# Two input matrices laid out by features on the host, row factors spread by products, and the residual input loaded late

## The chip, the cores and the metric

One core of one Trainium2 chip runs the whole program. The metric is the device time of one execution in microseconds (us); each version is run several times and the median is given.

## The reference

Two transformer blocks with T = 256 tokens and D = 1024 features run one after the other, in fp32. The change touches the opening of the first block only:

```python
hx = modulate(rms_norm(x, norm1_g[i]), sh1, sc1)      # x   [256, 1024]
hc = modulate(rms_norm(ctx, norm1_g[i]), csh1, csc1)  # ctx [256, 1024]
qx, kx, vx, ux = split_proj(hx @ w_in[i])
kvc = hc @ w_in[i][:, ATT_DIM:3 * ATT_DIM]
...
x_new = x + g1 * (jnp.concatenate([attn_x, conv_x], axis=-1) @ w_out[i])
```

`rms_norm` divides each token's row by the root of its mean square and multiplies by a gain per feature; `modulate(h, shift, scale)` is `h * (1 + scale) + shift`, where shift and scale come from `silu(c) @ w_ada + b_ada` (for ctx from c_ctx). So a token needs one factor (the "row factor") and a feature needs a factor and an addend.

## The kernel before

The program is one hand-written instruction stream per engine, tied by counting semaphores; an engine runs its own stream strictly in the order written. SyncE (`sync_program`) issues the weight loads through one queue in the order of `weight_units`, each when the ring slots that it overwrites have been read. TensorE (PE) multiplies. Weights are split in two fp32r parts: ScalarE (ACT) writes the high part WH (`high_halves`, called `hi`), VectorE (DVE) the low part WL (`low_halves`, called `lo`), and every product is three matmuls: high x high, high x WL, low activations x WH. The activations are split likewise into AH and AL (for x) and CH and CL (for ctx).

The opening works so. SyncE loads x by tokens (X, two blocks of 128 tokens on the partitions), then for e8 = 0 to 7 an 1 MB block of w_ada ("ada block") and a 0.5 MB block of w_in ("ab block"); ctx (XC) goes into the queue between ab block 6 and ada block 7; after ab block 7 follow the 1 MB blocks k0, k1, q0, q1, v0, v1. k0 may be issued when PE has read ada block 5, k1 when it has read ada block 7. ACT squares the rows of X with a sum along the row, GpSimd (POOL) raises mean + eps to -0.5 (`power`), DVE multiplies X by the row factor (`hat`) into S1. PE first runs 11 filler products of ones (`keep_busy`, L476, each two instructions), then `mod_first(0)` (L454, the ada product), `mod_turn(0)` (L465 transposes 2 blocks of S1, L468 the 2 row blocks of the modulation), 8 more filler products, and then the loop over e8: `mod_first(e8 + 1)`, `ab(e8, 0)`, `mod_turn(e8 + 1)`, `ab(e8, 1)` (L490 to L496). For each e8 DVE copies the modulation rows out (`rows_out`), sums and adds (`modulation`), applies factor and addend to the turned S1 in PSUM (`modulate_x`, L1538), writes WL of the ab block, and AL (`low_x`); ACT copies AH (`high_x`).

For ctx ACT squares XC after e8 = 5, DVE scales it (`hat`, L1493) into XC2 at e8 = 6 and once more between the low parts of k0 and k1. PE turns XC2 by `c_turns` (L396), twice two banks of four transposes, between the parts of the k product. DVE (`modulate_c0`) and ACT (`modulate_c(1)` to `(3)`, L1033) apply factor and addend out of PSUM.

Behind this DVE goes on in written order: low parts of q0 and q1, rope of K (KR), 20 taps of the depthwise convolution (L1496), low parts of v, 8 taps, rope of Q (QR, after ACT has copied Q out), 52 taps, and then the attention loop over u = 0 to 7. There `soft1` (L1666) adds bias and finds maxima, ACT takes the exponential, `norm1` (L1493) scales, PE turns the probabilities (`turn1`, L396), and `pv1(u)` (L598) multiplies by V into bank 5. `pv1(u)` takes that bank only when DVE has run `o1_lo(u - 1)` (L1490). In its loop DVE runs norm1(u), soft1 of u + 1, the tail of the modulation, some taps, then o1_lo(u - 1). Before `turn1(0)` PE runs the second half of the last v product, scores1(1) and two ada products.

Of the kernel before, what the change touches and what calls it, by code (L numbers as in the profile page):

```python
# [5 lines left out]
F32 = mybir.dt.float32  # L6
# [18 lines left out]
class Mem:  # L25


    def __init__(self, nc, ctx):
# [30 lines left out]
        def M(name, off, shape, dt=F32):  # L59
            return at(name, 121.75 + off, shape, dt)  # L60
# [10 lines left out]
        self.XC2 = M("XC2", 56, [128, 2, D])  # L71
# [69 lines left out]
x_hat mx_dve mx_act kx c_hat c_turned mc_dve mc_act kc  # L141
# [143 lines left out]
def sync_program(e, m, S, units, out, d):  # L285
    w = Waits(e)

    def load(n):
        unit = units[n]
        for old in unit.old:  # L290
            w.wait_ge(old.free[0], old.free[1])
        v = unit.block(m)
        for c0, cw, src in unit.pieces:
            e.dma_start(v[:, :, c0:c0 + cw], src).then_inc(unit.landing, 16)

    for tb in range(2):
        e.dma_start(m.X[:, tb, :], d["x"][128 * tb:128 * tb + 128, :]).then_inc(S[f"l_x{tb}"], 16)
    for n in range(14):
        load(n)
    e.dma_start(m.XC[:, :, :], d["ctx"].rearrange("(t p) n -> p t n", p=128)).then_inc(S["l_xc"], 16)  # L300
    for n in range(14, len(units)):
        load(n)
    for n in range(3):
        tb, c = n // 2, slice(512 * (n % 2), 512 * (n % 2) + 512)
        e.wait_ge(S["y_out"], n + 1)
        e.dma_start(out[tb * 128:tb * 128 + 128, c], m.S1[:, tb, c]).then_inc(S["l_out"], 16)
    e.wait_ge(S["l_out"], 64)
# [58 lines left out]
def tensor_program(e, m, S, by):  # L366
# [11 lines left out]
    def frees(b, *pairs):  # L378
        free[b] = [(S[sem], value) for sem, value in pairs]
# [79 lines left out]
    def mod_turn(e8):  # L459

        b = turn_bank("rows1_turned")
        w.wait_ge(S["l_id"], 16)
        w.wait_ge(S["x_hat"], 2)
        for tb in range(2):
            e.transpose(bank[b][:, 256 + tb * 128:384 + tb * 128], m.S1[:, tb, 128 * e8:128 * e8 + 128], m.ident[:, :])  # L465
        w.wait_ge(S["rows1_dve"], e8 + 1)
        for j in range(2):
            ins = e.transpose(bank[b][:, j * 128:j * 128 + 128], m.rows1[e8][:, j * 128:j * 128 + 128], m.ident[:, :])  # L468
        ins.then_inc(S["rows1_turned"], 1)
        frees(b, ("mx_dve", e8 + 1))  # L470
# [10 lines left out]
    def ab(e8, tb):  # L481

        unit = by["ab"][e8]
        wh, wl = m.WH[unit.slot], m.WL[unit.slot]
        hs = m.AH[:, e8, tb * 128:tb * 128 + 128]
        ls = m.AL[:, e8, tb * 128:tb * 128 + 128]
        w.wait_ge(S["mx_act"], e8 + 1)
        for n in range(2):
            w.wait_ge(S["w_hi"], unit.hi + n + 1)
            e.matmul(bank[2 * n + tb][:, :], hs, wh[:, 512 * n:512 * n + 512], start=e8 == 0, stop=False)  # L490
        for n in range(2):
            w.wait_ge(unit.lo[0], unit.lo[1] + n + 1)
            e.matmul(bank[2 * n + tb][:, :], hs, wl[:, 512 * n:512 * n + 512], start=False, stop=False)
        w.wait_ge(S["kx"], e8 + 1)
        for n in range(2):
            e.matmul(bank[2 * n + tb][:, :], ls, wh[:, 512 * n:512 * n + 512], start=False,  # L496
                     stop=e8 == 7).then_inc(S["b_mm" if n else "a_mm"], 1)

    keep_busy(11)
    mod_first(0)  # L500
    mod_turn(0)
    keep_busy(8)
    for e8 in range(8):
        if e8 < 7:
            mod_first(e8 + 1)
        ab(e8, 0)
        if e8 < 7:
            mod_turn(e8 + 1)
        ab(e8, 1)
    for tb in range(2):  # L510
        frees(tb, ("u", tb + 1))
        frees(2 + tb, ("gate_u", tb + 1))

    def c_turn(i):
        w.wait_ge(S["c_hat"], 2)
        b = turn(pair(m.XC2, 2 * i), "c_turned")
        frees(b, ("mc_act", 3 * i - 1) if i else ("mc_dve", 2))
# [6 lines left out]
    def c_turns(i):  # L524
        c_turn(i)
        c_turn(i + 1)

    def u_turns():
        u_turn(0)
# [3 lines left out]
    def c_ready(k):  # L533
        return "kc", k // 2 + 1

    product(by["k"], m.AH, m.AL, 0, 4, "k_mm", x_ready, 512, lambda: c_turns(0))
    frees(4, ("k_out", 1))
    c_turns(2)
    product(by["k"], m.AH, m.AL, 1, 5, "k_mm", x_ready, 512, u_turns)
    frees(5, ("k_out", 2))  # L540
    for tb in range(2):
# [447 lines left out]
def scalar_program(e, m, S, units, by, out, d):  # L989
# [32 lines left out]
    def high_x(k):  # L1022

        w.wait_ge(S["mx_dve"], k + 1)
        copy(m.AH[:, k, :], m.hT[:, k, :], "mx_act")

    def modulate_c(i, n):

        w.wait_ge(S["c_turned"], i + 1)
        w.wait_ge(S["mod1"], 16)  # L1030
        for k in (2 * i, 2 * i + 1):
            src = bank[m.turn_bank["c_turned", i + 1]][:, k % 2 * 256:k % 2 * 256 + 256]
            e.activation(m.hTc[:, k, :], src, ACT.Identity, bias=m.mod1[:, k, 0, 1:2],  # L1033
                         scale=m.A1[:, 1, k:k + 1]).then_inc(S["mc_act"], 1)
# [429 lines left out]
def vector_program(e, m, S, units, by):  # L1464
# [33 lines left out]
    def col(i):  # L1498
        return stat[:, i:i + 1]
# [777 lines left out]
```

## Time and profile before

| | us |
|---|---|
| median of 3 runs | 733.89 (733.76 to 734.76) |
| the profiled execution | 736.95 |
| its span | 735.1 |
| PE busy in the span | 722.5 |
| DVE busy in the span | 508.5 |
| ACT busy in the span | 397.8 |

All times of rows below are microseconds from the start of the span of the profiled execution. That execution took 3.06 us more than the median. PE stands still for 12.6 us in all, so the rows tell most at the few places where it does and where it nearly does.

### The profile page before, as it was taken

How to read it: one execution, taken by the hardware profiler on the slowest of the kernel's cores; microseconds unless marked ns; L12 is line 12 of the kernel's file. 1: busy time of each engine (PE TensorE's matmuls, PEld its weight loads, DVE VectorE, ACT ScalarE, POOL GpSimd, SP SyncE). 2: the span in 40 equal slices, each digit the busy share in tenths (PEclk: the TensorE clock that was granted, in tenths of full speed). 3: DMA queues.
4: the chain of work that ended last, by engine and by line, in shares of the span. 5: the costliest groups of instructions: out<-in, count | busy, mean ns of one | idle time of the engine just before them, and what ended most of it. 6: DMA issues, size and time to landing. Idle time of an engine off the chain costs nothing.

```text
span 735.1 us, 9749 instructions
## 1 busy us (share of the span) xinstructions
PE 722.5 (98%) x3806; PEld 577.7 (79%) x3806; DVE 508.5 (69%) x924; ACT 397.8 (54%) x662; POOL 24.9 (3%) x44
## 2 busy tenths in 40 slices
PE   7999999999999999999999999999999999999996
PEld 5668885568888888888878777778888888888885
DVE  3688999889667555565988799865857445544544
ACT  3366336886666545556545677666466344434432
POOL 1020011000100000000010000000000000000000
PEclk8999999999999999999999999999999999999999
DMA  9984939954464656545528533344366655655511
GB/s 366 385 325 172 364 114 357 370 171 165 162 221 167 229 182 215 172 157 190 160 96 302 203 116 115 118 171 170 115 230 203 197 173 189 206 177 171 173 58 57
DMA packets 73741, 144.90 MB, mean 197 GB/s; under 512 B 4112, under 2 KB 27664, under 8 KB 72672
## 3 DMA queue, kind: packets, MB, share of 16 engines
q1 hardware_dynamic: 71888, 138.98, 54.6%
q0 software_dynamic: 1520, 5.03, 1.9%
q8 instruction: 30, 0.49, 0.3%
q10 hardware_dynamic: 288, 0.27, 0.1%
q14 instruction: 15, 0.12, 0.0%
HBM read 143.22 MB, written 1.05 MB: 196 GB/s over the span
## 4 chain that ended last, share of the span: by engine, by line
PE 92%; DVE 3%; issue 2%; DMA 1%; ACT 1%; POOL 0%; SPq 0%; POOLq 0%; DVEq 0%
PE bank L414 22%; PE bank L416 22%; PE bank L415 22%; PE bank L734 5%; PE bank L396 5%; PE bank L732 3%; PE bank L433 2%; PE bank L454 1%; DMA W<-in_w_ada 1%; PE bank L576 1%; PE bank L490 1%; PE bank L598 1%; PE bank L851 1%; PE bank L873 1%; DVE WL L1481 1%
## 5 line engine op out<-in xcount | busy, mean ns | idle before, releaser
L1481 DVE TENSOR_TENSOR WL<-W,WH 128x1024 fp32r<-128x1024 f32 (+2 forms) x222 | 249.5, 1169 | 47.7 <-ACT WH L1004 47.4
L1004 ACT ACTIVATE WH<-W 128x1024 fp32r<-128x1024 f32 (+2 forms) x222 | 211.5, 1011 | 52.8 <-DMA W<-in_w_mlp 40.3
L414 PE MATMUL bank<-WH,AHL 128*128 128x512 f32 (+1 forms) x480 | 189.2, 394 | 0.3 <-DVE AHL L1490 0.3
L416 PE MATMUL bank<-WH,AHL 128*128 128x512 f32 (+1 forms) x480 | 185.4, 386 | 0.0
L415 PE MATMUL bank<-WL,AHL 128*128 128x512 f32 (+1 forms) x480 | 185.2, 386 | 0.0
L414 PEld LDWEIGHTS bank<-WH,AHL 128*128 128x128 f32 x480 | 90.2, 188 | 21.5 <-issue 3.2
L416 PEld LDWEIGHTS bank<-WH,AHL 128*128 128x128 f32 x480 | 90.2, 188 | 18.7
L415 PEld LDWEIGHTS bank<-WL,AHL 128*128 128x128 f32 x480 | 90.3, 188 | 16.9
L414 PE MATMUL bank<-WH,HH 128*128 128x512 f32 (+1 forms) x218 | 84.9, 390 | 0.0
L416 PE MATMUL bank<-WH,HL 128*128 128x512 f32 (+1 forms) x218 | 84.5, 388 | 0.0
L415 PE MATMUL bank<-WL,HH 128*128 128x512 f32 (+1 forms) x218 | 84.4, 387 | 0.0
L734 PE MATMUL bank<-AHL,WH 128*128 128x512 f32 x168 | 60.5, 398 | 0.0
L732 PE MATMUL bank<-AHL,WL 128*128 128x256 f32 x192 | 50.0, 281 | 0.0
L1496 DVE SCALAR_TENSOR_TENSOR cacc<-hp,vec,cacc 128x256 f32<-128x256 f32 x120 | 48.3, 475 | 0.0
L416 PEld LDWEIGHTS bank<-WH,HL 128*128 128x128 f32 x218 | 40.9, 188 | 8.5
L415 PEld LDWEIGHTS bank<-WL,HH 128*128 128x128 f32 x218 | 41.0, 188 | 8.3
L414 PEld LDWEIGHTS bank<-WH,HH 128*128 128x128 f32 x218 | 40.9, 188 | 8.0
L1413 ACT ACTIVATE rel<-bank 128x256 f32<-128x256 f32 x22 | 8.5, 384 | 62.2 <-PE bank L416 61.1
L1490 DVE TENSOR_TENSOR hid<-bank,rel 128x256 f32<-128x256 f32 x22 | 9.3, 424 | 42.2 <-ACT rel L1413 42.2
L732 PEld LDWEIGHTS bank<-AHL,WL 128*128 128x128 f32 x192 | 36.3, 189 | 2.0
L734 PEld LDWEIGHTS bank<-AHL,WH 128*128 128x128 f32 x168 | 31.6, 188 | 6.7
L1784 DVE TENSOR_TENSOR HL<-bank,HH 128x256 fp32r<-128x256 f32 (+1 forms) x26 | 11.1, 460 | 30.9 <-ACT HH L1012 30.9
(265 smaller groups left out, 829.5 us busy)
## 6 DMA issues: line engine op xcount, KB each, us to landing
W<-in_w_mlp SPq DMA_DIRECT2D x32, 1024.0 KB, 5.4
W<-in_w_in SPq DMA_DIRECT2D x24, 1024.0 KB, 5.1
W<-in_w_ada SPq DMA_DIRECT2D x12, 1024.0 KB, 7.5
WX<-in_w_ada SPq DMA_DIRECT2D x12, 1024.0 KB, 9.4
W<-in_w_gate SPq DMA_DIRECT2D x22, 512.0 KB, 4.1
W<-in_w_up SPq DMA_DIRECT2D x22, 512.0 KB, 5.3
W<-in_w_down SPq DMA_DIRECT2D x11, 1024.0 KB, 4.9
W<-in_w_out SPq DMA_DIRECT2D x8, 1024.0 KB, 5.0
```

The source lines that it names most:

```text
L396: ins = e.transpose(bank[b][:, c * 128:c * 128 + 128], src, m.ident[:, :])
L414: e.matmul(po, hs, wh[:, k, c0:c0 + cw], start=first and k == 0, stop=False)
L415: e.matmul(po, hs, wl[:, k, c0:c0 + cw], start=False, stop=False)
L416: ins = e.matmul(po, ls, wh[:, k, c0:c0 + cw], start=False, stop=last and k == unit.nk - 1)
L433: ins = e.matmul(bank[bk][32 * g:32 * g + 32, :], m.csp[:, k0 + g, :], wv[:, g, :], start=k0 == 0, stop=k0 == 4, tile_position=(0, 32 * g))
L732: ins = e.matmul(bank[4 + j][:, 0:256], wl[:, k, js], m.AH[:, 4 * i + k, :], start=False, stop=False)
L734: ins = e.matmul(both, wh[:, k, js], m.AHL[:, :, 4 * i + k, :], start=False, stop=i == 1 and k == 3)
L1004: e.activation(m.WH[unit.slot][:, c], m.W32[unit.slot][:, c], ACT.Copy).then_inc(S["w_hi"], 1)
L1481: e.tensor_tensor(m.WL[unit.slot][:, c], m.W32[unit.slot][:, c], m.WH[unit.slot][:, c].bitcast(F32), ALU.subtract).then_inc(S["w_lo"], 1)
L1490: e.tensor_tensor(o, a, b, op).then_inc(S[sem], 1)
L1496: e.scalar_tensor_tensor(o, a, scalar, b, op0, op1).then_inc(S[sem], 1)
L1784: e.tensor_tensor(L[:, k0:k0 + nj, ts], bank[b][:, 0:nj * 128].rearrange("p (j n) -> p j n", j=nj), H[:, k0:k0 + nj, ts].bitcast(F32), ALU ...
```

## The change

x and ctx are also laid out by features on the host (XT and CT: 128 partitions, 8 blocks, 256 tokens). At the start XT is loaded in two halves instead of X. ACT squares XT elementwise (no sum), and PE sums the squares over features by products with a column of ones: 16 products with one output column (`x_sums`), then `spread` brings the two row factors over all partitions by 2 products with the identity, and DVE copies them to rB. `modulate_x` reads XT and rB from SBUF and multiplies by factor and row factor; the addend is put in by ACT in `high_x` and by DVE in `low_x`. The two transposes of S1 in each `mod_turn` are gone. The filler is 6 products before x_sums, 4 between x_sums and spread, and 4 (was 8) behind mod_turn(0).

For ctx, XC still comes by tokens for the squares, and CT is loaded as well, between ab block 7 and k0. DVE's two scalings (`hat`) go; instead DVE, behind `u`, multiplies CT by the spread factors in PSUM (two operations of 128 x 1024), and `modulate_c0` and `modulate_c` read CT from SBUF. The four `c_turn`s of four transposes are gone from PE; one `spread` is added between ab(7, 0) and ab(7, 1). X by tokens is loaded behind v1, and `residual1` waits for it.

```diff
-    for tb in range(2):
-        e.dma_start(m.X[:, tb, :], d["x"][128 * tb:128 * tb + 128, :]).then_inc(S[f"l_x{tb}"], 16)
+    for h in range(2):
+        e.dma_start(m.XT[:, 4 * h:4 * h + 4, :], d["xt"][:, 4 * h:4 * h + 4, :]).then_inc(S[f"l_x{h}"], 16)
...
     for n in range(14, len(units)):
+        if n == 16:
+            e.dma_start(m.CT[:, :, :], d["ctxt"]).then_inc(S["l_ct"], 16)
+        if n == 22:
+            e.dma_start(m.X[:, :, :], d["x"].rearrange("(t p) n -> p t n", p=128)).then_inc(S["l_x"], 16)
         load(n)
...
-        w.wait_ge(S["x_hat"], 2)
-        for tb in range(2):
-            e.transpose(bank[b][:, 256 + tb * 128:384 + tb * 128], m.S1[:, tb, 128 * e8:128 * e8 + 128], m.ident[:, :])
...
-    keep_busy(11)
+    def x_sums():
+
+        for h in range(2):
+            w.wait_ge(S["sq_sum"], h + 1)
+            for k in range(4 * h, 4 * h + 4):
+                for tb in range(2):
+                    ins = e.matmul(bank[6 + tb][:, 0:1], m.xsq[:, k, tb * 128:tb * 128 + 128], m.ones[:, 0:1], start=k == 0,
+                                   stop=k == 7)
+        ins.then_inc(S["r_mm"], 1)
+
+    def spread(b, i):
+
+        w.wait_ge(S["l_id"], 16)
+        w.wait_ge(S["rstd"], i + 2)
+        for tb in range(2):
+            ins = e.matmul(bank[b][:, tb * 128:tb * 128 + 128], m.stat[:, 40 + i + tb:41 + i + tb].to_broadcast([128, 128]),
+                           m.ident[:, :], start=True, stop=True)
+        ins.then_inc(S["r_mm"], 1)
+
+    keep_busy(6)
+    x_sums()
+    keep_busy(4)
+    spread(turn_bank("x_spread", 6), 0)
+    frees(6, ("r_x", 1))
     mod_first(0)
     mod_turn(0)
-    keep_busy(8)
+    keep_busy(4)
...
+        else:
+            b = turn_bank("c_spread")
+            spread(b, 2)
+            frees(b, ("c_hat", 2))
...
-    product(by["k"], m.AH, m.AL, 0, 4, "k_mm", x_ready, 512, lambda: c_turns(0))
+    product(by["k"], m.AH, m.AL, 0, 4, "k_mm", x_ready)
     frees(4, ("k_out", 1))
-    c_turns(2)
     product(by["k"], m.AH, m.AL, 1, 5, "k_mm", x_ready, 512, u_turns)
...
-        copy(m.AH[:, k, :], m.hT[:, k, :], "mx_act")
+        e.activation(m.AH[:, k, :], m.hT[:, k, :], ACT.Identity, bias=m.mod1[:, k, 0, 0:1]).then_inc(S["mx_act"], 1)
...
-        square(tb, m.X[:, tb, :], m.S1[:, tb, :])
+        e.activation(half_of(m.xsq, tb), half_of(m.XT, tb), ACT.Square, scale=1.0 / 32).then_inc(S["sq_sum"], 1)
...
         if k == 6:
             mean_square(2, (2,))
-            hat(m.XC, m.XC2, 0, 2, "c_hat")
-    lo()
-    mean_square(3, (3,))
-    hat(m.XC, m.XC2, 1, 3, "c_hat")
-    lo()
+            mean_square(3, (3,))
+    lo(2)
     for tb in range(2):
         w.wait_ge(S["gate_u"], tb + 1)
         w.wait_ge(S["a_mm"], 15 + tb)
         tt(m.U[:, tb, :], bank[tb][:, :], m.G[:, tb, :], ALU.mult, "u")
+    w.wait_ge(S["r_mm"], 3)
+    w.wait_ge(S["l_ct"], 16)
+    for i in range(2):
+        cv = m.CT[:, 4 * i:4 * i + 4, :]
+        rv = bank[m.turn_bank["c_spread", 1]][:, 0:256]
+        tt(cv, cv, rv.unsqueeze(1).to_broadcast([128, 4, 256]), ALU.mult, "c_hat")
     modulate_c0()
```

## Rows read from the trace of the kernel before

**Rows 1.** The page, part 1: busy time and share of the span.

```profile
PE 722.5 (98%) x3806; PEld 577.7 (79%) x3806; DVE 508.5 (69%) x924; ACT 397.8 (54%) x662; POOL 24.9 (3%) x44
```

**Rows 2.** Windows: stretch, PE, PEld, DVE, ACT, POOL busy, PEclk, DMA share, GB/s.

```profile
9.00:10.00 1.00, 0.42 (x5) 0.26 (x9) 0.00 (x0) 0.00 (x0) 0.00 (x0) 0.54 1.09 451
...
15.00:16.00 1.00, 1.00 (x6) 0.85 (x5) 0.46 (x2) 0.67 (x2) 0.00 (x0) 0.55 0.94 385
...
42.00:46.00 4.00, 3.61 (x30) 2.12 (x28) 3.06 (x7) 2.95 (x5) 0.55 (x1) 1.00 0.37 93
```

**Rows 3.** Timeline of PE, opening: start, duration, engine, line, operation.

```profile
9.57 1.94 PE L454 MATMUL bank<-W,csp 128*32 128x256 f32 x16 [2.72 <-DMA W<-in_w_ada]
...
12.53 3.56 PE L476 MATMUL bank<-ones 128*128 128x128 f32 x16
```

**Rows 4.** Timeline of ACT, the second square of X.

```profile
5.42 1.04 ACT L1016 ACTIVATE S<-X 128x1024 f32<-128x1024 f32 x1
```

**Rows 5.** Timeline of POOL, the power of one row factor.

```profile
5.85 0.56 POOL L317 TENSOR_TENSOR stat<-stat 128x1 f32<-128x1 f32 x1 [3.15 <-DVE stat L1507]
```

**Rows 6.** The chain of waits: start, us on the chain, what.

```profile
53.84 0.87 PE bank L396 x8
...
155.97 0.54 PE bank L639 x4
```

**Rows 7.** Timeline of PE: ada block 7, ab(7, 0), k product, turn1(0), pv1(1).

```profile
42.52 1.07 PE L454 MATMUL bank<-WX,csp 128*32 128x256 f32 x16
...
47.90 0.73 PE L490 MATMUL bank<-WH,AHL 128*128 128x512 f32 x2 [0.29 <-ACT AHL L1012]
...
50.95 0.40 PE L414 MATMUL bank<-WH,AHL 128*128 128x512 f32 x1
...
115.91 1.09 PE L396 MATMUL bank<-ident,s 128*128 128x128 f32 x8
...
125.37 0.66 PE L598 MATMUL bank<-PT,V 128*64 128x128 f32 x8
```

**Rows 8.** Timeline of DVE from U to o1_lo(0).

```profile
54.87 1.28 DVE L1490 TENSOR_TENSOR U<-bank,G 128x512 f32<-128x512 f32 x2
...
67.08 1.22 DVE L1490 TENSOR_TENSOR KR<-Kt,rope 128x1024 f32<-128x1024 f32 x1 [0.20 <-ACT Kt L1012]
...
87.14 1.23 DVE L1490 TENSOR_TENSOR QR<-Q,rope 128x1024 f32<-128x1024 f32 x1 [0.60 <-ACT Q L1012]
...
90.88 20.68 DVE L1496 SCALAR_TENSOR_TENSOR cacc<-hp,vec,cacc 128x256 f32<-128x256 f32 x52
...
114.47 0.49 DVE L1493 TENSOR_SCALAR s<-s,rl 128x512 f32<-128x512 f32 x1
...
124.94 0.28 DVE L1490 TENSOR_TENSOR AHL<-bank,AHL 128x128 fp32r<-128x128 f32 x1
```

**Rows 9.** Timeline of ACT: WH of k0 and k1, modulate_c(3), WH of q0 and q1.

```profile
47.76 3.89 ACT L1004 ACTIVATE WH<-W 128x1024 fp32r<-128x1024 f32 x4
...
59.54 1.01 ACT L1033 ACTIVATE hTc<-bank,mod,A 128x256 f32<-128x256 f32 x2
...
61.11 3.89 ACT L1004 ACTIVATE WH<-W 128x1024 fp32r<-128x1024 f32 x4
```

**Rows 10.** DMA issues one by one, us to landing: ada block 7, k0, k1.

```profile
WX<-in_w_ada SPq DMA_DIRECT2D x1, 1024.0 KB, 10.6
...
W<-in_w_in SPq DMA_DIRECT2D x1, 1024.0 KB, 9.8
...
W<-in_w_in SPq DMA_DIRECT2D x1, 1024.0 KB, 5.1
```

**Rows 11.** Timeline of SyncE's queue and one issue's source: when issued.

```profile
30.23 0.47 SPq L294 DMA_DIRECT2D WX<-in_w_ada  x1
...
L294 SPq DMA_DIRECT2D W<-in_w_in x1: 379/379/379, 34.9 to 34.9; - x1
...
L294 SPq DMA_DIRECT2D W<-in_w_in x1: 379/379/379, 43.7 to 43.7; - x1
```

More of the change, by code:

```diff
@@ L70, in __init__ @@
         self.XC = M("XC", 48, [128, 2, D])
-        self.XC2 = M("XC2", 56, [128, 2, D])
+        self.CT = M("CT", 56, [128, 8, 256])
+        self.XJ = M("XJ", 64, [128, 2, D])
+        self.XT = M("XT", 0, [128, 8, 256])
+        self.xsq = M("xsq", 24, [128, 8, 256])
+        self.rB = M("rB", 72, [128, 256])
         self.hTc = M("hTc", 0, [128, 8, 256])
@@ L140 @@
 sq_sum mean_sq rstd ada1_mm rows1_dve rows1_turned mod1_sum mod1
[L141 removed]
+r_mm r_x l_x l_ct mx_dve mx_act kx c_hat mc_dve mc_act kc
 a_mm b_mm gate_u u u_turned hp conv_first conv k_mm q_mm v_mm k_out kc_out q_out v_out vc_out rope_mul kr qr qk_turned qk_act
@@ L469, in mod_turn @@
         ins.then_inc(S["rows1_turned"], 1)
-        frees(b, ("mx_dve", e8 + 1))
+        frees(b, ("mod1_sum", e8 + 1))
     def keep_busy(count):
@@ L512, in tensor_program @@
         frees(2 + tb, ("gate_u", tb + 1))
[L514 to L517, printed above, removed]
     def u_turn(j):
@@ L522, in u_turn @@
         frees(b, ("hp", j + 1))
-    def c_turns(i):
-        c_turn(i)
-        c_turn(i + 1)
     def u_turns():
@@ L1024, in high_x @@
         w.wait_ge(S["mx_dve"], k + 1)
-        copy(m.AH[:, k, :], m.hT[:, k, :], "mx_act")
+        e.activation(m.AH[:, k, :], m.hT[:, k, :], ACT.Identity, bias=m.mod1[:, k, 0, 0:1]).then_inc(S["mx_act"], 1)
     def modulate_c(i, n):
-        w.wait_ge(S["c_turned"], i + 1)
-        w.wait_ge(S["mod1"], 16)
+        w.wait_ge(S["c_hat"], 2)
+        w.wait_ge(S["mx_dve"], 8)
         for k in (2 * i, 2 * i + 1):
-            src = bank[m.turn_bank["c_turned", i + 1]][:, k % 2 * 256:k % 2 * 256 + 256]
-            e.activation(m.hTc[:, k, :], src, ACT.Identity, bias=m.mod1[:, k, 0, 1:2],
+            e.activation(m.hTc[:, k, :], m.CT[:, k, :], ACT.Identity, bias=m.mod1[:, k, 0, 1:2],
                          scale=m.A1[:, 1, k:k + 1]).then_inc(S["mc_act"], 1)
@@ L1039, in two, with half_of @@
         return hT[:, 2 * i:2 * i + 2, :].rearrange("p a b -> p (a b)")
+    def half_of(t, h):
+        return t[:, 4 * h:4 * h + 4, :].rearrange("p a b -> p (a b)")
     e.dma_start(m.cs[:, :], d["cs"]).then_inc(S["l_cs"], 16)
@@ L1051, in scalar_program @@
     for tb in range(2):
-        square(2 + tb, m.XC[:, tb, :], m.XC2[:, tb, :])
+        square(2 + tb, m.XC[:, tb, :], m.XJ[:, tb, :])
     hi()
@@ L1537, in modulate_x @@
         w.wait_ge(S["mod1"], 2 * k + 2)
-        e.tensor_scalar(m.hT[:, k, :], bank[m.turn_bank["rows1_turned", k + 1]][:, 256:512], m.A1[:, 0, k:k + 1],
-                        m.mod1[:, k, 0, 0:1], ALU.mult, ALU.add).then_inc(S["mx_dve"], 1)
+        w.wait_ge(S["r_x"], 1)
+        w.wait_ge(S[f"l_x{k // 4}"], 16)
+        fused(m.hT[:, k, :], m.XT[:, k, :], m.A1[:, 0, k:k + 1], m.rB[:, :], ALU.mult, ALU.mult, "mx_dve")
     def low_x(k):
@@ L1544, in low_x @@
         w.wait_ge(S["mx_act"], k + 1)
-        tt(m.AL[:, k, :], m.hT[:, k, :], m.AH[:, k, :].bitcast(F32), ALU.subtract, "kx")
+        fused(m.AL[:, k, :], m.hT[:, k, :], m.mod1[:, k, 0, 0:1], m.AH[:, k, :].bitcast(F32), ALU.add, ALU.subtract, "kx")
     def modulate_c0():
         w.wait_ge(S["mod1"], 16)
-        w.wait_ge(S["c_turned"], 1)
+        w.wait_ge(S["c_hat"], 2)
         for k in range(2):
-            e.tensor_scalar(m.hTc[:, k, :], bank[m.turn_bank["c_turned", 1]][:, k * 256:k * 256 + 256], m.A1[:, 1, k:k + 1],
+            e.tensor_scalar(m.hTc[:, k, :], m.CT[:, k, :], m.A1[:, 1, k:k + 1],
                             m.mod1[:, k, 0, 1:2], ALU.mult, ALU.add).then_inc(S["mc_dve"], 1)
@@ L1566, in vector_program @@
     e.tensor_copy(m.csp[:, :, 0:2], m.cs[:, :].rearrange("p (k r) -> p k r", r=2)).then_inc(S["csp"], 1)
+    w.wait_ge(S["r_mm"], 1)
     for tb in range(2):
-        mean_square(tb, (tb,))
-        hat(m.X, m.S1, tb, tb, "x_hat")
+        e.tensor_scalar(col(24 + tb), bank[6 + tb][:, 0:1], EPS, None, ALU.add).then_inc(S["mean_sq"], 1)
+    w.wait_ge(S["r_mm"], 2)
+    e.tensor_copy(m.rB[:, :], bank[6][:, 0:256]).then_inc(S["r_x"], 1)
     for k in range(8):
@@ L1792, in residual1 @@
         hn = slice(512 * n, 512 * n + 512)
+        w.wait_ge(S["l_x"], 16)
         w.wait_ge(S["out_mm"], OUT_AT[n, tb])
@@ L2230, in fm, with blocks @@
         return v.reshape(-1, 128).T
+    def blocks(v):
+        return v.T.reshape(8, 128, 256).transpose(1, 0, 2)
     bada = a["b_ada"].reshape(-1)
@@ L2260 @@
     arrays = {
-        "vec": vec, "cs": cs, "x": a["x"][0], "ctx": a["ctx"][0], "ident": np.eye(128, dtype=np.float32),
+        "vec": vec, "cs": cs, "x": a["x"][0], "ctx": a["ctx"][0], "xt": blocks(a["x"][0]), "ctxt": blocks(a["ctx"][0]), "ident": np.eye(128, dtype=np.float32),
         "rope1": rope_tables(lambda t: (t // 64, t % 64), 32), "rope2": rope_tables(lambda t: (t,), 64),
```

## Prediction

> **What bounds the kernel now.** I read the page's busy times first: PE works 722.5 us of 735.1 [rows 1], so an edit pays only if it takes work off PE or closes one of its few holes, and only as long as no other engine becomes late. Then I read the timelines of PE, ACT, POOL and DVE over the first 126 us, with the windows for clock and DMA. The opening shows a hole of 2.72 us before the first ada product, which waits for its block [rows 3]; within it the granted clock falls to 1.2 GHz (0.54 is the mean of the microsecond from 9, so it fell at 9.1), and it is back at 2.4 GHz from 15.9 (0.55 from 15 to 16) [rows 2]. From there PE is busy to 111 us but for 0.39 us between 42 and 46 [rows 2] and 0.29 before 47.9 [rows 7], 0.7 together. What the page doesn't tell is how late the other engines are. DVE starts the attention stage directly out of its 52 taps, which run from 90.88 for 20.68 us, that is to 111.56 [rows 8]. Its first normalised probabilities are ready at 114.47 + 0.49 = 114.96; PE turns them at 115.91 [rows 7, 8]: 0.95 us of slack. Its o1_lo(0) ends at 124.94 + 0.28 = 125.22, and pv1(1), which needs it, starts at 125.37 [rows 7, 8]: 0.15 us. So at 125 us DVE is as much the bound as PE, and whatever PE gains before is kept only as far as DVE comes earlier too. That is the core of this forecast.
>
> **The change on PE.** Gone at 2.4 GHz: 16 transposes of S1 and 16 of ctx. Eight cost 0.87 us [rows 6], 0.109 each: 3.5 us, of which the pair in mod_turn(0) ran at 1.2 GHz and cost twice. Gone at 1.2 GHz: 4 of 8 filler products, 3.56/8 = 0.445 each [rows 3], 1.8 us. Gone as well are 0.7 us of holes at e8 = 7 behind the scaling of XC. Added: one spread at e8 = 7, 4 instructions of 0.109, 0.45 us, and the opening's 16 one-column products. Each is 2 instructions; four such instructions (L639) took 0.54 us with their tail [rows 6], the transposes say 0.109: 32 cost 3.5 to 4.3 us at 2.4 GHz, double at 1.2. The second half starts only when ACT's second square is done at 5.42 + 1.04 = 6.5 [rows 4]; the first half may not be through by then.
>
> The opening, at 2.4 GHz throughout: one-column products end near 9.1; DVE adds eps, POOL takes two powers of 0.56 [rows 5], about 10.5; spread 0.45; the first ada product starts at 10.9 (was 9.57), but takes 1.0 instead of 1.94, and with 4 fast filler products the second starts at 13.6 (was 16.02). At e8 = 1 PE is 2.6 us ahead, and each step gives 0.22 more. By e8 = 7 it wants ada block 7 at 38.1 (was 42.52 [rows 7]). That block was issued at 30.23 and landed at 40.8 [rows 10, 11], and the DMA engines are full in the opening (a share of 0.94 to 1.09, 385 to 451 GB/s [rows 2]), so it can't come much sooner: 40.2 I take. The rest of the loop takes 50.95 - 42.52 = 8.43 us less the 0.7 of holes and 0.22, plus 0.45: 8.0. PE reaches the k product at 48.2 (was 50.95), waits a little for k0's low part (48.6), and loses the four c_turns: 2.35 + 1.74 = 4.1 us ahead until turn1(0).
>
> **The change on DMA, ACT and DVE.** CT puts 1 MB ahead of k0. Between 42 and 46 us only 93 GB/s flowed [rows 2], at 400 that leaves room for 1.2 MB, so CT fills a hole: k0 (issued at 34.9, landed 44.7 [rows 10, 11]) comes about 2 us later, k1 (43.7, landed 48.8 [rows 10, 11]) about when it did. Its issue waits for ada block 7's product and so moves up 2.3 us, while the hole in front is gone: between 48.2 (all of the hole used) and 51.4 (CT's 2.6 us added in full); I take 48.5. X, another 1 MB, is issued behind v1 and so lies in front of nothing but the later ada blocks; at the start XT's 1 MB takes X's place. Both cost nothing.
>
> ACT needs 0.97 us for each half of k1 [rows 9], so its high part is ready at 50.45 (was 51.65). DVE's last low part takes 1.2, as KR's product of the same size does [rows 8]: 51.65. U: 1.28 for two [rows 8]: 52.9. Now the new operations: CT times factors, 128 x 1024 with one operand in PSUM, twice. U costs 0.64 for 512 elements a partition, so 1.28 for one at most, and 1.22 at least, which KR's product of 1024 elements took out of SBUF; I take 2.45 in all: 55.4. This is added to the chain, since ACT's three modulate_c, which began at 54.76 before, now wait for it. One takes 61.11 - 59.54 = 1.57 [rows 9], with CH behind; three 4.75: ACT begins q0's high part at 60.15 (was 61.11). DVE's two old scalings and its waits for POOL's powers are gone, which is why DVE isn't later. The fused forms of modulate_x and low_x are the operation of the taps at the same size, 20.68/52 = 0.40 each [rows 8]; I cost them at nothing, the loop over e8 hides them while it waits for its block, and 0.1 each would move A by less than 0.1. All later steps of DVE follow ACT by the old distance: KR at 66.1 (was 67.08 [rows 8]). QR waited 0.60 for ACT's copy of Q [rows 8]; PE is 4.1 us early there, so that wait goes.
>
> **Sum.** DVE at 111.5: 0.95 + 0.60 = 1.55 us earlier. At turn1(0) PE may gain 1.55 + 0.95 = 2.5; at pv1(1) 1.55 + 0.15 = 1.7. PE has 4.1, so it stands about 1.6 us before turn1(0) and 0.8 more by pv1(1), and **1.7 us** is what is left. Behind this PE's steps are longer than DVE's, the slack grows, and the gain stays. The profiled execution would take 736.95 - 1.7 = 735.25; the median, 3.06 lower, 732.2.
>
> **The rivals.** (A, forecast, 0.42) As above, 732.2, with k1's landing and the two products with the factors as unknowns: 731.3 to 732.9.
>
> (B, 0.32) The opening stays at 1.2 GHz for longer. There is less filler, one-column products keep PE little occupied, and before 9 us the clock was lost while PE stood [rows 2, 3]. Then the spread and the first ada product cost double, the first starts at 11.7, ends at 13.6, and e8 = 0 is done 1 to 2 us later than it was; ada block 7 is asked for near 42, k1 is issued at 43 and lands at 49.5. DVE is then 0.55 early at 111.5, the gain is 0.7: 733.2. The clock of 10 to 20 us decides between A and B. The Trainium skill (TensorE: Matmul & The Clock Gate, Part 1) says that "the default state is throttled, and activity releases the throttle". By that rule taking filler out speaks for B; the rows agree in that the clock fell in the hole and came back behind eight filler products.
>
> (C, 0.06) DVE isn't the bound I take it for; PE keeps all of its 4.1 us: 729.8. Against it stands the slack of 0.15 us [rows 7, 8].
>
> (D, 0.11, slower) The new hole before turn1(0), 1.6 us here and more if DVE comes later, takes the clock down, as the hole of 2.72 us did [rows 3], and PE runs at 1.2 GHz for a stretch as long as then, 6.8 us from 9.1 to 15.9 [rows 2]. That costs half of it, 3.4 us, on a PE-bound stage: -1.7 + 3.4 = +1.7, 735.6. It decides once the hole comes near the old one's length.
>
> (E, 0.09, slower) CT doesn't fit into the hole, k1 lands at 51.4. All of ACT's and DVE's chain is 2.9 us later than in A: 735.1. It turns into a loss from a landing at 50.2 on.
>
> **How the numbers follow.** A measurement of this kernel can tell 0.2% from no change, 1.47 us; the limits are 732.4 and 735.4. A reaches to both sides of the lower limit: 0.30 of its 0.42 below it. Faster 0.30 + 0.06 and 0.02 from B: 0.38. Slower: D and half of E, with a little for costs that I have not seen, 0.18. The rest, 0.44, is no change. The range takes in A, B and E and the cheaper end of D: 731.0 to 735.4.
>
> **What would show it.** Right: ada block 7's product waits for its block near 40; k1 lands at 48 to 49.5; the new products of DVE lie at about 53 to 55.4 with 1.17 to 1.28 each; ACT starts q0's high part near 60; QR without a wait; PE idle before turn1(0) with DVE as the releaser, and again before pv1(1). Wrong: PE without a hole at 112 us, DVE at its taps until 111.5 or later, a clock under 1.0 behind 20 us, or k1's landing past 50. If the opening is at 1.2 GHz to 19 us, B holds.

## The result: 7.4 us slower, and the profile after

The changed kernel takes 741.25 us (median of 4 runs, 740.38 to 743.04) against 733.86 (733.76 to 734.76): a ratio of 1.0098, 95% interval 1.0085 to 1.0111. The forecast was 732.2, its range 731.0 to 735.4. The profiled execution took 741.68 us, its span is 739.9. That is 4.7 us more than the profiled one of before (736.95), which was itself 3.06 above its median.

The page after, parts 1 and 4 (the chain's share of the span by engine); before, PE's share of the chain was 92% and DVE's 3%.

```profile
PE 726.8 (98%) x3804; PEld 581.2 (79%) x3804; DVE 508.3 (69%) x923; ACT 398.6 (54%) x660; POOL 24.6 (3%) x44
...
PE 82%; DVE 11%; ACT 3%; issue 2%; DMA 1%; POOL 0%; POOLq 0%; DVEq 0%; SPq 0%
```

PE executes two instructions fewer and is busy 4.3 us longer; DVE's part of the chain has grown fourfold. PE's timeline after, opening and attention stage:

```profile
2.76 2.93 PE L481 MATMUL bank<-ones 128*128 128x128 f32 x12 [2.76 <-POOL ones L342]
6.12 6.99 PE L510 MATMUL bank<-ones,xsq 128*128 128x1 f32 x32 [0.43 <-ACT xsq L1070]
12.97 2.05 PE L481 MATMUL bank<-ones 128*128 128x128 f32 x8
...
15.81 1.94 PE L462 MATMUL bank<-W,csp 128*32 128x256 f32 x16
...
20.69 1.92 PE L462 MATMUL bank<-WX,csp 128*32 128x256 f32 x16
...
25.76 1.07 PE L462 MATMUL bank<-W,csp 128*32 128x256 f32 x16
...
119.80 1.09 PE L404 MATMUL bank<-ident,s 128*128 128x128 f32 x8 [1.74 <-DVE s L1517]
...
130.15 0.66 PE L620 MATMUL bank<-PT,V 128*64 128x128 f32 x8 [0.30 <-DVE AHL L1514]
```

The first ada product starts at 15.81 (was 9.57), the second at 20.69 (was 16.02, behind the 3.56 us of filler [rows 3]). Both take 1.9 us, the third 1.07: PE ran at 1.2 GHz up to some 22.5 us, and no fall follows before the last 5 us of the span. The windows' PEclk column says 1.00 all through that opening, since it knows no earlier level than the first recorded change; the durations of equal work tell the level.

DVE and ACT after, from U to turn1(0)'s source; the answering rows are [rows 8, 9]:

```profile
55.79 2.36 DVE L1505 TENSOR_TENSOR WL<-W,WH 128x1024 fp32r<-128x1024 f32 x2 [0.86 <-ACT WH L1026]
58.07 1.28 DVE L1514 TENSOR_TENSOR U<-bank,G 128x512 f32<-128x512 f32 x2
59.27 2.34 DVE L1514 TENSOR_TENSOR CT<-CT,bank 128x1024 f32<-128x1024 f32 x2
...
72.57 1.23 DVE L1514 TENSOR_TENSOR KR<-Kt,rope 128x1024 f32<-128x1024 f32 x1 [0.19 <-ACT Kt L1034]
...
91.94 1.22 DVE L1514 TENSOR_TENSOR QR<-Q,rope 128x1024 f32<-128x1024 f32 x1
...
95.67 20.67 DVE L1520 SCALAR_TENSOR_TENSOR cacc<-hp,vec,cacc 128x256 f32<-128x256 f32 x52
...
119.25 0.49 DVE L1517 TENSOR_SCALAR s<-s,rl 128x512 f32<-128x512 f32 x1
```

```profile
54.70 2.01 ACT L1026 ACTIVATE WH<-W 128x1024 fp32r<-128x1024 f32 x2 [1.21 <-DMA W<-in_w_in]
...
61.64 1.09 ACT L1054 ACTIVATE hTc<-CT,mod,A 128x256 f32<-128x256 f32 x2 [3.96 <-DVE CT L1514]
...
66.60 3.89 ACT L1026 ACTIVATE WH<-W 128x1024 fp32r<-128x1024 f32 x4
```

The reader is to see three steps. ACT waits for k1 until 54.70, where it had landed at 48.8 [rows 10, 11]: 5.9 later. 4.2 of them come from ada block 7's product, which k1's issue waits for and which starts at 46.75 instead of 42.52 [rows 7]; the other 1.7 go with CT ahead of k1 in the queue (tested below). So U starts 3.2 later than before. The two products with the factors add 2.34, so KR is 5.5 late. QR no longer waits (it had 0.60), the taps are 4.8 late, and turn1(0), which had 0.95 of slack, is 3.9 late and waits 1.74 for DVE. From its start to the end of the span it is another 620.1, before 619.2 [rows 7]; two more new waits, 0.48 before an ada product and the 0.30 before pv1(1), make up nearly all of that difference.

### The profile page after: what moved, and what is told of

Read it like the earlier page. It is cut to its first block, busy times and chain, and to the rows that moved or that the text cites. A ratio compares the mean times of both kernels' runs of the same rounds, so it can differ in the third digit from the quotient of the medians.

```text
span 739.9 us, 9751 instructions
## 1 busy us (share of the span) xinstructions
PE 726.8 (98%) x3804; PEld 581.2 (79%) x3804; DVE 508.3 (69%) x923; ACT 398.6 (54%) x660; POOL 24.6 (3%) x44
## 4 chain that ended last, share of the span: by engine, by line
PE 82%; DVE 11%; ACT 3%; issue 2%; DMA 1%; POOL 0%; POOLq 0%; DVEq 0%; SPq 0%
PE bank L422 20%; PE bank L424 19%; PE bank L423 19%; PE bank L756 5%; DVE cacc L1520 5%; PE bank L404 4%; PE bank L754 3%; DVE WL L1505 1%; PE bank L462 1%; PE bank L441 1%; PE bank L510 1%; PE bank L495 1%; DMA W<-in_w_in 1%; PE bank L873 1%; PE bank L895 1%
```

## The experiments

Theory at the start: (1) the opening at 1.2 GHz costs most; (2) DVE, not PE, carries the delay into the attention stage; (3) CT and its products add to DVE's chain. Rivals: the freed hole and its clock (D), and that PE alone sets the time. The kernel before was measured again beside each group of experiments (734.05 to 734.24 us); the ratios are to that. The name in brackets behind a result is the one by which later expectations call the version.

### Sums with 128 output columns

```diff
-                    ins = e.matmul(bank[6 + tb][:, 0:1], m.xsq[:, k, tb * 128:tb * 128 + 128], m.ones[:, 0:1], start=k == 0,
+                    ins = e.matmul(bank[6 + tb][:, 0:128], m.xsq[:, k, tb * 128:tb * 128 + 128], m.ones[:, 0:128], start=k == 0,
```

> The changed kernel with one size altered: the 16 products that sum the squares multiply by 128 columns of ones instead of 1 (same number of instructions and of weight loads). Theory (the one-column products don't count as work for the clock, so PE stays at 1.2 GHz until 22.5 us, and everything starts late): the clock rises during or soon after these products, which then take 3.5 to 5 us instead of 6.99, the first ada product starts near 12 to 13.5 (15.81), DVE's 52 taps start 2 to 4 us earlier than 95.67, and the time falls by 2 to 4 us against the changed kernel. Rival (the shorter filler ahead of them lost the clock, the columns don't matter): the clock still rises at 22 us and the time is that of the changed kernel within 0.7 us.

Measured (e1_wide): 736.92 us (736.37 to 739.54, 10 runs), 1.0034 of before (1.0023 to 1.0045): 4.3 less than the changed kernel, a little more than the 2 to 4 expected. PE's timeline of this kernel, and two windows (PEclk is the number ahead of the last two):

```profile
6.11 3.85 PE L510 MATMUL bank<-ones,xsq 128*128 128x128 f32 x32 [0.42 <-ACT xsq L1070]
...
12.15 1.07 PE L462 MATMUL bank<-W,csp 128*32 128x256 f32 x16
...
15.09 1.07 PE L462 MATMUL bank<-WX,csp 128*32 128x256 f32 x16
...
114.38 1.09 PE L404 MATMUL bank<-ident,s 128*128 128x128 f32 x8 [2.13 <-DVE s L1517]
```

```profile
115.00:116.00 1.00, 1.00 (x9) 0.74 (x9) 1.00 (x4) 1.00 (x3) 0.77 (x2) 0.69 1.06 397
117.00:119.00 2.00, 2.00 (x12) 0.20 (x8) 2.00 (x6) 0.93 (x2) 0.00 (x0) 0.55 1.05 388
```

The 32 instructions took 3.85 us, and the first ada product is 3.7 us earlier, at full clock. DVE's 52 taps start at 90.25, 5.4 earlier (expected 2 to 4). Nine of its ten executions lie within 1 us. So the larger part of the loss lies in the opening. Rival D's mechanism appears too: a hole of 2.13 us, then 1.2 GHz from 115.4 to 118.8.

### More filler, or far fewer one-column products

```diff
-    keep_busy(6)
+    keep_busy(11)
```

> The changed kernel with the 11 filler products of the kernel before ahead of the sums instead of 6. Rival (filler was what the clock lacked): the clock rises near 6 us as in the kernel before, the one-column products take 3.5 us, the time falls by 2 to 4 us. Theory (one-column products don't count): the clock may rise at the end of the filler but falls again during the one-column products, which start at 6.9 to 7.6 us; the first ada product starts between 13 and 17 us, and the time changes by less than 1.5 us.

Measured (e2_filler): 738.63 us (737.09 to 738.75, 4 runs), 1.0045 (1.0028 to 1.0062), 2.6 less than the changed kernel. PE's opening and a window:

```profile
7.62 3.90 PE L510 MATMUL bank<-ones,xsq 128*128 128x1 f32 x32
...
14.23 1.43 PE L462 MATMUL bank<-W,csp 128*32 128x256 f32 x16
...
12.00:14.00 2.00, 2.00 (x10) 1.87 (x9) 0.00 (x0) 0.25 (x1) 0.96 (x2) 0.50 1.03 422
```

With the clock up from 8.2, soon after they began, the one-column products take 3.90 us, inside the 3.5 to 4.3 of the forecast. But behind them, with PE busy throughout, the clock is down from 11.6 to 15.0. The theory had this fall right and the time wrong: it allowed less than 1.5 us, and the 2.6 lie in the rival's 2 to 4. So the shorter filler is part of the cause beside the one-column products; with it back the clock came up at 8.2 instead of 22.5.

In the next one DVE adds the eight blocks first, and PE needs only 2 one-column products:

```diff
...
+        w.wait_ge(S["xs"], 5)
+        for tb in range(2):
+            ins = e.matmul(bank[6 + tb][:, 0:1], m.xsq[:, 0, tb * 128:tb * 128 + 128], m.ones[:, 0:1], start=True, stop=True)
```

> The changed kernel, but DVE, which idles there, adds the 8 feature blocks of the squares first (5 additions, about 1.6 us of them behind ACT's last square), and PE needs 2 one-column products instead of 16. Theory (the 7 us of the sums stand on the path of the opening): the sums end near 10 us (13.11), the first ada product starts at 12 to 13 (15.81), DVE's 52 taps start about 3 us earlier than 95.67, and the time falls by about 3 us. Rival (the opening is hidden behind the loads of the ada blocks): the time falls by less than 1 us.

Measured (e3_presum): 737.46 us (736.37 to 738.68, 8 runs), 1.0039 (1.0027 to 1.0051). PE waits 3.58 us for DVE, and its first ada product still runs at 1.2 GHz:

```profile
9.27 1.01 PE L508 MATMUL bank<-ones,xsq 128*128 128x1 f32 x4 [3.58 <-DVE xsq L1511]
...
12.99 1.92 PE L462 MATMUL bank<-W,csp 128*32 128x256 f32 x16
```

It is 3.8 us faster than the changed kernel although PE stands idle: the 7 us of slow instructions cost more than a hole of 3.58.

### Is DVE the bound? Narrow taps, in both kernels

```diff
+            cw = 128 if 36 <= n < 84 else 256
-            fused(m.cacc[:, c, :], m.hp[:, c, j:j + 256], m.dw[:, c, j:j + 1], m.cacc[:, c, :], ALU.mult, ALU.add, "conv")
+            fused(m.cacc[:, c, 0:cw], m.hp[:, c, j:j + cw], m.dw[:, c, j:j + 1], m.cacc[:, c, 0:cw], ALU.mult, ALU.add, "conv")
```

> The changed kernel with 48 of the 52 taps before the attention stage on 128 of their 256 columns (so half of these taps' work is left out and the convolution is not the reference's): some 6.4 us less work for DVE between 95.7 and 116. Theory (behind the opening DVE alone carries the delay into the attention stage; PE is only 2.1 us late at its turns of K and Q, 104.7 against 102.63): the hole of 1.74 us before turn1(0) goes, PE is the bound, and the time falls by 2.3 to 3.0 us. Rival (DVE's taps lie beside work that is as late): the time falls by less than 1 us.

48 of the 52 taps leave out half of their columns, so the convolution isn't the reference's. Measured in the changed kernel (e4_narrow): 737.29 us (737.13 to 738.98, 6 runs), 4.0 less (expected 2.3 to 3.0). DVE's taps take 14.27 instead of 20.67, and turn1(0) no longer waits:

```profile
94.41 14.27 DVE L1520 SCALAR_TENSOR_TENSOR cacc<-hp,vec,cacc 128x256 f32<-128x256 f32 x52
...
116.36 1.09 PE L404 MATMUL bank<-ident,s 128*128 128x128 f32 x8
```

Not all of it is DVE's: in this execution the clock was up from 17.4, and PE reached the turns of K at 103.08, after 104.71 in the changed kernel. Of the 4.3 between the two profiled executions 1.6 belong to the opening, and 1.74 + 0.48 + 0.30 = 2.5 are the waits that went. The clock didn't fall behind turn1(0).

> The kernel before with 48 of the 52 taps on 128 of 256 columns, as in e4_narrow (half of these taps' work left out). It says what 6.4 us less of DVE's work is worth where the opening isn't late. Theory (in the kernel before PE and DVE are level at the attention stage, slack 0.15 to 0.95 us): the time changes by less than 0.7 us, so the 4.0 us that the same cut gave in the changed kernel are lateness that DVE carried. Rival (DVE bounds the kernel before as well): the time falls by over 2 us.

The same edit in the kernel before (e8_narrow_before): 735.37 us (733.79 to 737.09, 10 runs), 1.001 (0.9998 to 1.0021). The median is 1.3 above before's, outside the 0.7 expected; the profiled execution (735.39) had its clock down from 10.4 to 13.8 in the opening, and from turn1(0)'s start to the end of its span it takes 619.2, as before. 6.4 us off DVE bring nothing where PE isn't waiting for it. The pair shows that DVE bounds the changed kernel and not the one before.

### The hole before turn1(0)

On top of the wide sums, 8 filler products stand in the hole:

```diff
+        if n == 0:
+            fb = 6 + turns["n"] % 2
+            take(fb)
+            for _ in range(8):
+                e.matmul(bank[fb][:, 0:128], m.ones[:, :], m.ones[:, :], start=True, stop=True)
```

> The kernel of e1_wide with 8 filler products (1.8 us at 2.4 GHz) in the hole before turn1(0), into the bank that turn1(0) writes next. In e1_wide PE stood 2.1 us there and the clock was at 1.2 GHz from 115.4 to 118.8. Theory (the hole takes the clock down, and that costs half of the 3.4 us): no stretch at 1.2 GHz behind 20 us, the time falls by 1.2 to 1.8 us against e1_wide (736.9), to about 735.4. Rival (PE at 1.2 GHz there waits for DVE anyway): the time stays within 0.5 us of e1_wide.

Measured (e5_hole): 736.17 us (735.85 to 739.44, 10 runs), 1.0039 (1.0024 to 1.0053). By the medians that is 0.75 less than without the filler; by the ratios (1.0039 for 1.0034) it isn't less, since four of the ten executions are slow for another reason. The clock stays up behind the filler. With PE no longer slowed, pv1(1) waits for DVE where it had no wait. And the opening of the profiled execution (738.77) is a slow one, though its sums have 128 columns:

```profile
6.19 6.60 PE L510 MATMUL bank<-ones,xsq 128*128 128x128 f32 x32 [0.50 <-ACT xsq L1075]
...
127.25 0.66 PE L625 MATMUL bank<-PT,V 128*64 128x128 f32 x8 [0.29 <-DVE AHL L1519]
```

What the fall costs is read from the profiled executions. From turn1(0)'s start to the end of the span they take 619.2 to 619.3 us without a hole (before, and five experiments), 620.1 with a hole, or the filler in it, and the clock kept (the changed kernel, this one and one below), and 620.7 to 620.8 with a hole and the clock down (four). So the fall costs about 0.7, not the 3.4 that rival D charged and not the 1.2 to 1.8 expected here: a PE that waits for DVE anyway loses little by being slow. As to the opening, six of the ten executions lie between 735.85 and 736.25, four between 738.77 and 739.44. With the 739.54 of the version without the filler, five of twenty executions with wide sums are some 3 us slower than the rest, and with one-column sums seven of eight (the x part alone, below). So wide sums seem to make the slow opening rarer; they don't exclude it. Only one of the five was profiled.

### Each half alone

The kernel before with the ctx part only (`CT` ahead of k0, one `spread`, no `c_turns`):

```diff
+        if n == 16:
+            e.dma_start(m.CT[:, :, :], d["ctxt"]).then_inc(S["l_ct"], 16)
...
-    product(by["k"], m.AH, m.AL, 0, 4, "k_mm", x_ready, 512, lambda: c_turns(0))
+    product(by["k"], m.AH, m.AL, 0, 4, "k_mm", x_ready)
     frees(4, ("k_out", 1))
-    c_turns(2)
```

> The kernel before with the part on ctx alone (CT loaded between ab block 7 and k0, DVE multiplies it behind U, no c_turns, one spread); x is as before. Theory (DVE's new 2.34 us and the later k blocks are on the chain that leads through the taps into the attention stage, PE's 1.74 us are not): DVE's 52 taps start later than in the kernel before by 1 to 2.5 us, a hole opens before turn1(0), the time is 735 to 737.5, slower than before. Rival (all of the loss comes from x's sums in the opening): the time is 732 to 734.

Measured (e6_c_only): 735.73 us (735.02 to 739.2, 11 runs) against 734.05, 1.0014 (1.0004 to 1.0024): 1.7 slower by the medians, 0.3 to 1.8 by the interval. The profiled execution is the slowest, 739.2: PE ran at 1.2 GHz up to about 15.5, though the opening is the old one. Its second ada product starts at 15.83, that of before's profile at 16.02, so the rows of the two can be compared. ACT's timeline, two rows of DVE, and the windows in which the hole of before lay [rows 2]:

```profile
51.50 2.01 ACT L1010 ACTIVATE WH<-W 128x1024 fp32r<-128x1024 f32 x2 [2.57 <-DMA W<-in_w_in]
...
58.45 1.10 ACT L1038 ACTIVATE hTc<-CT,mod,A 128x256 f32<-128x256 f32 x2 [3.97 <-DVE CT L1495]
...
52.59 2.36 DVE L1486 TENSOR_TENSOR WL<-W,WH 128x1024 fp32r<-128x1024 f32 x2 [2.20 <-ACT WH L1010]
54.87 1.28 DVE L1495 TENSOR_TENSOR U<-bank,G 128x512 f32<-128x512 f32 x2
...
42.00:44.00 2.00, 2.00 (x21) 1.02 (x20) 2.00 (x7) 1.76 (x3) 0.14 (x1) 1.00 1.02 402
44.00:46.00 2.00, 2.00 (x13) 1.65 (x12) 0.66 (x4) 1.19 (x3) 0.92 (x2) 1.00 0.88 254
```

CT does flow into the hole: 402 and 254 GB/s where 93 had been the mean. Yet k1 comes at 51.5 where 48.8 had been: 2.7 later, the time of 1 MB at 390 GB/s. ada block 7's product starts no later here (42.31 for 42.52). That is the landing of rival E (51.4). Still U starts at 54.87, just as before [rows 8]: DVE's two scalings are gone, and the wait of 2.20 for k1 takes the time that they left free. The two products behind U, 2.34, then come on top, and KR starts 2.3 later than before.

The x part only (the changed kernel with ctx as before):

```diff
-        if n == 16:
-            e.dma_start(m.CT[:, :, :], d["ctxt"]).then_inc(S["l_ct"], 16)
...
-    product(by["k"], m.AH, m.AL, 0, 4, "k_mm", x_ready)
+    product(by["k"], m.AH, m.AL, 0, 4, "k_mm", x_ready, 512, lambda: c_turns(0))
     frees(4, ("k_out", 1))
+    c_turns(2)
```

> The changed kernel with ctx treated as before (XC scaled by DVE, c_turns on PE, no CT): the part on x alone. Theory (the opening costs most, the part on ctx 1 to 2.5 us more): 738.5 to 740.5 against 741.3. Rival (ctx costs nothing or helps PE): 741 or more.

Measured (e7_x_only): 739.35 us (735.52 to 741.3, 8 runs) against 734.05, 1.006 (1.0042 to 1.0079): 5.3 slower, and very uneven. The eight lie in three groups: one at 735.5, five from 738.5 to 739.5, two at 741.1 and 741.3. The profiled one is the fastest, and shows why:

```profile
6.12 3.88 PE L507 MATMUL bank<-ones,xsq 128*128 128x1 f32 x32 [0.43 <-ACT xsq L1074]
...
12.71 1.26 PE L459 MATMUL bank<-W,csp 128*32 128x256 f32 x16
...
15.85 1.07 PE L459 MATMUL bank<-WX,csp 128*32 128x256 f32 x16
```

Its clock was up at 6.3, just after the one-column products began, and they took 3.88; in the changed kernel's they took 6.99 with the same instructions before them. The two parts, 5.3 + 1.7 = 7.0, make up all but 0.4 of the 7.4.

### Where CT's load and products should stand

CT's load moved behind k1, all else as in the ctx part alone:

```diff
-        if n == 16:
+        if n == 18:
```

> The kernel of e6_c_only (before with the part on ctx) with CT's load moved behind k1. In e6_c_only k1 landed at 51.48 (48.78 before), ACT waited 2.57 us for it and DVE 2.20 us. Theory (CT in front of the k blocks is one half of what the part on ctx costs, DVE's 2.34 us of new work the other): k1 lands near 49, U starts 1.5 to 2.5 us earlier than 54.87, and the time falls by 1 to 2 us against e6_c_only (735.7). Rival (only DVE's added work costs): the time stays within 0.5 us of 735.7.

Measured (e9_c_ctlate): 733.62 us (732.97 to 737.18, 11 runs) against 734.24, 0.9986 (0.9972 to 1.0000), 2.1 less than with the load ahead of k0 (expected 1 to 2). The profiled execution, 733.35, has a fast opening (second ada product at 12.79), so its rows are earlier than those above by that too. DVE's low parts and PE's two waits:

```profile
45.15 4.62 DVE L1486 TENSOR_TENSOR WL<-W,WH 128x1024 fp32r<-128x1024 f32 x4
...
111.42 1.09 PE L399 MATMUL bank<-ident,s 128*128 128x128 f32 x8 [0.51 <-DVE s L1498]
...
121.77 0.66 PE L604 MATMUL bank<-PT,V 128*64 128x128 f32 x8 [0.29 <-DVE AHL L1495]
```

The low parts of k0 and k1 run in one piece, without a wait.

The other cure leaves CT ahead of k0 and puts DVE's products with the factors between the low parts of k0 and k1, where DVE waits:

```diff
-    lo(2)
+    lo()
...
+    lo()
```

> The kernel of e6_c_only with DVE's two multiplications of CT moved from behind U to between the low parts of k0 and k1, where DVE stood 2.20 us waiting for k1. Theory (the 2.34 us count only because of where they stand): they fill the wait, DVE's 52 taps start 1.5 to 2.3 us earlier than in e6_c_only, the time is 732.5 to 734.2, level with the kernel before or under it. Rival (DVE isn't what e6_c_only loses by): 735.2 or more.

Measured (e10_c_early): 733.99 us (733.71 to 734.56, 11 runs), 0.9994 (0.9985 to 1.0003), 1.7 less than the ctx part alone. The products cost nothing there, but PE's k product waits for the low part:

```profile
48.84 2.34 DVE L1495 TENSOR_TENSOR CT<-CT,bank 128x1024 f32<-128x1024 f32 x2
...
52.37 0.50 PE L417 MATMUL bank<-WH,AHL 128*128 128x512 f32 x1 [1.52 <-DVE WL L1486]
```

The whole change with every cure (wide sums, the first ada product directly behind them, the modulation's first copy ahead of rB's, the products with the factors early):

```diff
+            ins = e.matmul(bank[6 + tb][:, 0:128], m.xsq[:, k, tb * 128:tb * 128 + 128], m.ones[:, 0:128], start=k == 0,
...
-    keep_busy(4)
+    mod_first(0)
...
+    rows_out(0)
```

> The changed kernel whole, with three orders altered: the products that sum the squares take 128 columns of ones (as in e1_wide), the first ada product stands directly behind them instead of behind 4 filler products and the spread (DVE copies its rows out ahead of rB), and the multiplications of CT stand between the low parts of k0 and k1 (as in e10_c_early). Theory (the change loses by the sums ahead of the first ada product at 1.2 GHz and by DVE's work in the wrong place, not by its idea): the first ada product starts near 10 us (15.81), the time is 731.5 to 734.5. Rival (the host layout can't pay here): 736 or more.

Measured (e11_all_early): 734.84 us (734.61 to 735.39, 11 runs), 1.0002 (0.9993 to 1.0012). 6.4 of the 7.4 us are recovered, nothing is gained on before, and the expected 731.5 to 734.5 is missed. Its turn1(0) starts at 113.77, that of the version above, whose opening is the old one, at 112.92. The second ada product, 14.70 for 12.85, puts it 1.85 behind; the `mod_turn`s without S1 give back 7 x 0.22 = 1.5; and PE waits 2.0 instead of 1.5 for the low parts. So even with the clock up from about 7.7, within the sums (4.56 us here), they and the spread cost as much as the transposes that they replace.

Last, four taps moved from ahead of the attention loop into its third and fourth passes, with CT loaded late:

```diff
-    taps(52)
+    taps(48)
...
-        taps((9, 8, 8, 7, 4, 0, 0, 0)[u])
+        taps((9, 8, 10, 9, 4, 0, 0, 0)[u])
```

> The kernel before with the ctx part, CT loaded behind k1, and four of the 52 taps moved from before the attention loop to its third and fourth passes (two each). If DVE is the bound at turn1(0) and pv1(1), the two waits of the version without the shift (0.51 and 0.29 us) go, and the time falls by 0.5 to 0.9 us against its 733.62: about 732.9, 0.9984 of before or a little less. Rival: the two waits are only inferred and PE's work in front of them would take as long anyway; then 733.6 again. A third way: the taps come back in the later passes as new waits of PE for DVE, and the time is 733.6 or above, with waits for DVE behind 130 us in PE's timeline.

Measured (e12_late_shift): 733.14 us (732.79 to 734.95, 11 runs) against 734.16, 0.9987 (0.9977 to 0.9997): the only version whose interval lies below 1. The two waits are gone, and one has come back a pass later:

```profile
112.74 1.09 PE L399 MATMUL bank<-ident,s 128*128 128x128 f32 x8
...
128.38 0.66 PE L604 MATMUL bank<-PT,V 128*64 128x128 f32 x8 [0.51 <-DVE AHL L1495]
```

That it beats the version without the shift isn't shown; their ratios agree (0.9987 and 0.9986).

## Why the prediction was wrong

**The step that failed is the opening.** Its "one-column products end near 9.1" and "the first ada product starts at 10.9" took a clock of 2.4 GHz throughout; measured were 13.1 and 15.81, and the second at 20.69 for 13.6. Rival B (0.32) named the mechanism, "one-column products keep PE little occupied", and the rule of the Trainium skill (TensorE: Matmul & The Clock Gate, Part 1) that activity releases the throttle stood beside it. In the trace PE is busy from 2.76 on but for 0.43 and 0.64 us, and the clock comes up only at 22.5, so being busy as the timeline shows it didn't release it here. But B was priced at one or two microseconds at e8 = 0, when the products alone, at 0.218 us an instruction, take 7.0 for 3.5, and everything behind them to 22.5 runs at half speed as well. With the same sums at 128 columns the time fell by 4.3, with the filler ahead of them put back by 2.6. A price "double at 1.2" stood in the text; it was never carried through B's sum.

**The baseline hid part of it.** I took 3.06 off the forecast for the profiled execution, as if that surplus were a constant. It wasn't: before's profiled execution had its clock down from 9.1 to 15.9, and the kernels with the old opening whose clock held (the two with CT late and with the products early) start the second ada product at 12.8, not at 16.02. 733.35 and 734.0 are their profiled times. Against an opening that usually costs nothing, one that was already slow in the row looked cheap to change. The old opening isn't safe either: in four of its six profiles (before, the ctx part, the narrow taps in before and the last version) the clock was down for a part of it. The median execution of before was not profiled, but each execution's mean granted clock is on record. Of the 27 executions of before beside the versions with CT late, with the products early and with every cure, the 16 fastest (733.76 to 734.42) have 0.997 to 1.000, and the next seven (734.83 to 735.72) 0.995. That speaks for a clock that holds in the median one; where in an execution it was down, the mean doesn't show.

**CT in the DMA hole failed too.** "CT fills a hole" and k1 landing "about when it did" (48.5) took a mean of 93 GB/s over 4 us as room. The room was there and was used: from 42 to 48 us the ctx part alone moved 2.1 MB where before moved 1.2. Still k1 came 2.7 us late; why catching up on bytes did not bring k1 back in time isn't settled. Rival E (0.09) had it at 51.4, and 51.5 was measured there, with ada block 7's product where it had been; in the changed kernel it was 54.7. The forecast had DVE no later because its "two old scalings" are gone; in the ctx part alone the wait for k1 used up what they gave, and the two new products came on top. The cure was not to fill the hole but to stand behind k1.

**What held.** DVE as the bound at the attention stage: the two products 2.34 (forecast 2.45), QR's wait gone, turn1(0) waiting for DVE, pv1(1) again (0.30, forecast 0.8), and narrow taps that help the changed kernel and not the one before. The slack rule worked with the sign reversed: DVE 4.8 later, less 0.95 of slack, gives the 3.9 by which turn1(0) moved. C, in which DVE isn't the bound, is excluded by the same rows. That the wait at turn1(0), 1.74, lies beside the forecast's 1.6 is luck: PE was to be 4.1 early there and DVE 1.55, and they were 2.1 and 4.8 late. One number of the working doesn't follow from its terms: 2.6 us ahead and six more steps of 0.22 put ada block 7's product at 38.6, not 38.1; nothing hung on it, since the block was taken to land at 40.2.

**Rival D** happened in four experiments and not in the changed kernel (its hole was 1.74), and cost 0.7 for the 3.4 charged. The error was to call the stage PE-bound right where PE had just been found waiting for DVE.

Open: how the loss of the opening divides between the one column and the shorter filler; why the opening of one kernel is slow in one execution and not in another, with the same instructions; what keeps k1 late; and 0.4 of the 7.4 us, which lie within the intervals.

## What to carry to other kernels

A product with one column costs what one with 128 does here, and in an opening it has to be priced at the low clock, along with all that follows until the clock is up. Before subtracting "profiled less median", look whether the profiled execution's clock stretch is part of that difference, and compare both sides with the clock held. Work freed on the fullest engine is worth only the slack of the next one, here 0.95 us, so look first at where a load or 2.3 us of DVE work stands (2.1 and 1.7 us here): with the products well placed, taking 16 transposes of ctx off PE brought nothing that can be told from before (0.9994, 0.9985 to 1.0003).

## What the runs showed of the hardware

- 32 instructions of 128 x 1 take as long as 32 of 128 x 128: 3.88 and 3.85 us with the clock at 2.4 GHz for nearly all of the time, 6.99 at 1.2. The Trainium skill (TensorE: Matmul & The Clock Gate, Part 2, "LDWEIGHTS") has a weight load's time go by the columns of the stationary operand, 128 in both; the equal times fit that, but no run here varies those columns.
- All four profiles of an opening with 16 one-column products show 1.2 GHz behind them: to 22.5 (the changed kernel), to 17.4 (narrow taps), from 11.6 to 15.0 (more filler) and from 9.7 to 13.2 (x part alone); with DVE's presum and 2 such products it is to 14.8. With 128 columns the clock came up at 6.2, 7.7 and 12.0 in three profiles and held to the attention stage. The old opening, with more filler and no sums, shows 1.2 GHz too: from 9.1 to 15.9 (before), 10.4 to 13.8, 10.9 to 14.2 and up to 15.5 in four profiles; in two it held.
- The Trainium skill (the same page, Part 1) says that the moment of release varies between executions of one kernel. Profiles of kernels with the same instructions up to there agree: 22.5 and 17.4 (one column), 6.2 and 12.0 (128 columns). The price was larger than I had expected: the x part alone ranged from 735.52 to 741.3, though only its fastest execution was profiled.
- Holes of 2.05 to 2.13 us before turn1(0) were followed by 3.4 us at 1.2 GHz in four profiles; those of 1.74 and 0.51 weren't.
